# Down product of a float32 decoder trunk: two more pairs multiplied with seven products, four pairs with their lows made by an adding DMA

## The reference, cut to what matters

```python
def swiglu(h, w_gate, w_up, w_down):
    return (jax.nn.silu(h @ w_gate) * (h @ w_up)) @ w_down
# per layer i:
x = x + mixed                       # attention part
h = rmsnorm(x, ffn_norm[i])
x = x + swiglu(h, ffn_w_gate[i], ffn_w_up[i], ffn_w_down[i])
```

## Time and profile before

| what | value |
|---|---|
| median of 3 runs | 2079.42 us (2079.38 to 2079.92) |
| the profiled execution, its own time | 2080.89 us |
| its span | 2079.1 us |
| PE, DVE, ACT, POOL busy, share of the span | 100%, 85%, 70%, 5% |
| granted TensorE clock | 1.0 in the whole span |
| down product of layer 0 | 781.1 to 1012.3 us |
| down product of layer 1 | 1844.4 to 2075.3 us |

### The profile page before, as it was taken

One profiled execution on the slowest core, in us unless ns is written; L12 is line 12 of the kernel. 1 busy time (PEld: TensorE's weight loads), 2 busy tenths in 40 slices (PEclk: granted clock), 3 DMA queues, 4 the chain that ended last, 5 costly groups with the idle time before them and its releaser, 6 DMA issues.

```text
span 2079.1 us, 28758 instructions
## 1 busy us (share of the span) xinstructions
PE 2073.4 (100%) x9652; PEld 1712.0 (82%) x9652; DVE 1764.8 (85%) x2367; ACT 1462.7 (70%) x1993; POOL 99.9 (5%) x79
## 2 busy tenths in 40 slices
PE   9999999999999999999999999999999999999999
PEld 8888888888888888888888888888888888888887
DVE  5775658899999999999767677777999999999998
ACT  6677647677887777766657676666787788777665
POOL 1111000000000000000010101000000000000000
PEclk9999999999999999999999999999999999999999
DMA  8686547787888786665667777676788788876654
GB/s 286 214 229 190 172 164 219 218 260 238 236 254 253 232 237 216 209 207 182 213 217 222 244 211 246 223 226 222 230 240 258 233 240 245 251 223 212 207 184 157
DMA packets 340217, 463.68 MB, mean 223 GB/s; under 512 B 134576, under 2 KB 137360, under 8 KB 340112
## 3 DMA queue, kind: packets, MB, share of 16 engines
q1 hardware_dynamic: 333936, 441.31, 66.5%
q0 software_dynamic: 6080, 20.99, 6.2%
q10 hardware_dynamic: 96, 0.03, 0.0%
HBM read 408.27 MB, written 2.10 MB: 197 GB/s over the span
## 4 chain that ended last, share of the span: by engine, by line
PE 98%; ACT 1%; DMA 1%; DVE 0%; issue 0%; ACTq 0%; POOLq 0%
PE acc L2079 16%; PE work L2079 16%; PE work L2081 16%; PE work L2080 16%; PE acc L2081 16%; PE acc L2080 16%; PE work L2260 1%; PE work L2298 1%; DMA low_b<-raw 1%; PE work L2210 0%; PE work L2271 0%; ACT w_hi L1347 0%; PE work L2305 0%; PE acc L2068 0%; DVE w_lo L1649 0%; PE work L2274 0%
## 5 line engine op out<-in xcount | busy, mean ns | idle before, releaser
L1649 DVE TENSOR_TENSOR w_lo<-raw,w_hi 128x1024 fp32r<-128x1024 f32 x716 | 807.0, 1142 | 84.0 <-ACT w_hi L1347 78.2
L1347 ACT ACTIVATE w_hi<-raw 128x1024 fp32r<-128x1024 f32 x716 | 691.8, 990 | 224.2 <-PE work L2081 132.7
L2079 PE MATMUL work<-w_hi,xT_hi 128*128 128x512 f32 x1194 | 464.9, 389 | 0.0
L2081 PE MATMUL work<-w_hi,xT_lo 128*128 128x512 f32 x1194 | 464.6, 389 | 0.0
L2080 PE MATMUL work<-w_lo,xT_hi 128*128 128x512 f32 x1194 | 464.5, 389 | 0.0
L1347 ACT ACTIVATE w_hi<-sums 128x1024 fp32r<-128x1024 f32 x210 | 220.6, 1059 | 189.5 <-PE work L2081 123.4
L2079 PE MATMUL acc<-w_hi,xT_hi 128*128 128x512 f32 (+1 forms) x905 | 352.4, 389 | 0.5 <-DVE w_lo L1649 0.5
L2081 PE MATMUL acc<-w_hi,xT_lo 128*128 128x512 f32 (+1 forms) x905 | 349.0, 386 | 0.0
L2080 PE MATMUL acc<-w_lo,xT_hi 128*128 128x512 f32 (+1 forms) x905 | 349.0, 386 | 0.0
L1649 DVE TENSOR_TENSOR w_lo<-sums,w_hi 128x1024 fp32r<-128x1024 f32 x210 | 252.9, 1220 | 33.1 <-ACT w_hi L1347 32.5
L2079 PEld LDWEIGHTS work<-w_hi,xT_hi 128*128 128x128 f32 x1194 | 224.1, 188 | 47.0 <-DVE w_lo L1649 0.4
(11 more groups left out here) (209 smaller groups left out, 2438.9 us busy)
## 6 DMA issues: line engine op xcount, KB each, us to landing
raw<-in_ffn_w_down_dram SPq DMA_DIRECT2D x176, 512.0 KB, 4.7
raw<-in_ffn_w_gate_dram SPq DMA_DIRECT2D x160, 512.0 KB, 4.3
raw<-in_ffn_w_up_dram SPq DMA_DIRECT2D x160, 512.0 KB, 5.2
raw<-in_odd_w_in_dram SPq DMA_DIRECT2D x48, 1024.0 KB, 5.6
raw<-in_even_w_in_dram SPq DMA_DIRECT2D x32, 1024.0 KB, 5.9
raw<-in_even_w_out_dram SPq DMA_DIRECT2D x16, 1024.0 KB, 5.0
raw<-in_odd_w_out_dram SPq DMA_DIRECT2D x16, 1024.0 KB, 7.3
low_a<-raw POOLq DMA_DIRECT2D x20, 512.0 KB, 5.8
```

What stands on the lines that cost most here:

```text
L1347: act.activation(w_hi[:, s, 0:out], src, ACT.Copy).then_inc(hi_ready, 1)
L1649: dve.tensor_tensor(w_lo[:, s, 0:out], src, w_hi[:, s, 0:out].bitcast(F32), ALU.subtract).then_inc(lo_ready, 1)
L2079: pe.matmul(out_ps, x_hi, wh, start=start, stop=False)
L2081: return pe.matmul(out_ps, x_lo, wh, start=False, stop=stop)
```

## The change

`DOWN_SEVENS` gets one more pair in layer 0's first pass and one more in layer 1's second pass, and several of the others move. A new list `DOWN_ADDED` names four plain pairs (6 and 15 of layer 0's first pass, 5 and 14 of layer 1's second pass) that are done with `added_half`. Their highs and lows lie in the lower halves of `xT_hi` and `xT_lo`. The ring's splits no longer run at a fixed distance: `high` and `low` map each half to the split that is due there, and halves of added pairs take none. All three tables of due times are new (left out below but for their first lines).

```diff
-PARTS = {"seven": ("two", "one", "sums_a", "sums_b"), "eight": ("pair", "pair"), "last": ("first", "second")}
+PARTS = {"seven": ("two", "one", "sums_a", "sums_b"), "eight": ("pair", "pair"), "added": ("pair", "pair"), "last": ("first", "second")}
...
-DOWN_SEVENS = (((5, 8, 11, 14, 16, 18, 21), (9, 11, 13, 15, 18)), ((5, 8, 11, 14, 16, 18, 21), (5, 8, 11, 13, 15, 18)))
+DOWN_SEVENS = (((5, 8, 10, 12, 14, 17, 19, 21), (9, 11, 13, 15, 18)), ((5, 8, 11, 14, 16, 18, 21), (4, 7, 9, 11, 13,
+               16, 18)))
+DOWN_ADDED = (((6, 15), ()), ((), (5, 14)))
...
+NEGATE_DOWN = ((-8, 0), (-6, 1), (-5, 2), (-4, 3))
...
+        down_hi = xT_hi[:, 0:8, :].rearrange("p (t a) s -> p t (a s)", t=2)
+        down_lo = [xT_lo[:, 4 * i:4 * i + 4, :].rearrange("p a s -> p (a s)") for i in range(2)]
...
+                at_once = [starts[p][q] + i for p in range(2) for q, of in enumerate(DOWN[layer][p]) if of == "added" for i in range(2)]
+                length = starts[1][-1] + len(PARTS["last"])
+                ring = [at for at in range(length) if at not in at_once]
+                kinds = [kind for pairs in DOWN[layer] for of in pairs if of != "added" for kind in PARTS[of]]
+                turns = [at - SPLIT for at in range(SPLIT)] + ring
+                high = {turns[i] + 1: kind for i, kind in enumerate(kinds + AHEAD * ["plain"])}
+                low = {at + 1: kind for at, kind in high.items()}
+
                 def jobs(h, base, raw):
 
 
+                    for p in range(2):
+                        for q in DOWN_ADDED[layer][p]:
+                            for at, step in NEGATE_DOWN:
+                                if starts[p][q] + at == h:
+                                    k = DOWN_PAIRS * p + q
+                                    negate(k, step, raw + 2 * k - n.raw.c, True)
+                                    if step == 3:
+                                        e.passed()
...
                 for i, (q, of, cols) in enumerate(rest):
-                    pair_chunk(layer, q, cols, of, sum(r for r, _ in before[-RAW:]) - 2, (w_down, w_down))
-                    before.append((len(PARTS[of]), False))
+                    added = sum(by_dma for _, by_dma in before[1 - RAW:]) if before[-RAW][1] else None
+                    pair_chunk(layer, q, cols, of, sum(r for r, _ in before[-RAW:]) - 2, (w_down, w_down), added=added, by_dma=of == "added")
+                    before.append((0 if of == "added" else len(PARTS[of]), of == "added"))
...
-                pool.dma_start(added_lo[i][:, :].bitcast(F32), raw[:, (FIRST_SLOT + k) % RAW, i * HALF:(i + 1) * HALF],
+                pool.dma_start((down_lo if down else added_lo)[i][:, :].bitcast(F32), raw[:, (FIRST_SLOT + k) % RAW, i * HALF:(i + 1) * HALF],
                                accum_op=ALU.add).then_inc(low_added[i], 16)
...
-                    act.activation(added_lo[i][:, :], src, ACT.Copy, scale=-1.0).then_inc(negated, 1)
+                    act.activation((down_lo if down else added_lo)[i][:, :], src, ACT.Copy, scale=-1.0).then_inc(negated, 1)
                 else:
-                    act.activation(added_hi[:, i, :], src, ACT.Copy).then_inc(rounded, 1)
+                    act.activation((down_hi if down else added_hi)[:, i, :], src, ACT.Copy).then_inc(rounded, 1)
...
-            def added_half(i, kt, start, held):
+            def added_half(i, kt, start, held, staged, begins):
...
                 pe.wait_ge(low_added[i], n.lows.value(1, unit=16))
+                if staged is None:
+                    x_hi, x_lo, his, los = xT_hi[:, kt, :], xT_lo[:, kt, :], added_hi, added_lo
+                else:
+                    x_hi, x_lo, his, los = stage_hi[:, 2 * staged + kt, :], stage_lo[:, 2 * staged + kt, :], down_hi, down_lo
+                    if begins:
+                        pe.wait_ge(slo_ready, n.taken.value(1))
```

More of the change, by code:

```diff
@@ L293, in decoder_kernel @@
     HALVES = (4 + 8 * 8 + 2 * 4 * 8 + 3 * CG * 8 + 2 * (2 * 8 + (FB - 1) * len(RING))
-              + sum(len(PARTS[of]) for passes in DOWN for half in passes for of in half))
+              + sum(len(PARTS[of]) for passes in DOWN for half in passes for of in half if of != "added"))
     assert DOWN_PAIRS == FK // 2 and all(passes[0][-1] == "seven" for passes in DOWN) and FB % 2
@@ L738, in make_sums, with negate @@
                         n.sums.c += 1
-                def negate(k, step, more):
-                    e.negate(k, step, more)
+                def negate(k, step, more, down=False):
+                    e.negate(k, step, more, down)
                     if step < 2:
@@ L851, in jobs @@
                             if sum_at[u][step] == h:
-                                before = starts[units[u - 1][0]][units[u - 1][1]] + len(PARTS["seven"]) if u else 0
-                                make_sums(step, h + AHEAD - before, raw + 2 * (DOWN_PAIRS * p + q) - n.raw.c)
+                                before = ring.index(starts[units[u - 1][0]][units[u - 1][1]]) + len(PARTS["seven"]) if u else 0
+                                make_sums(step, sum(at <= h for at in low) - before, raw + 2 * (DOWN_PAIRS * p + q) - n.raw.c)
                         if form_at[u][3] == h:
@@ L876, in down @@
                                 e.direct_out(1, 0)
-                            ahead = dict(hi=kinds[h + AHEAD], lo=kinds[h + AHEAD - 1], staged=n.taken.c % STAGED, begins=i == 0)
+                            ahead = dict(hi=high.get(starts[p][0] + h), lo=low.get(starts[p][0] + h), staged=n.taken.c % STAGED, begins=i == 0)
                             if what == "seven":
@@ L883, in down @@
                                 half(kt=i, start=(q, i) == (0, 0), held=(q, i) == (0, 0),
-                                     direct_stop=p == 0 and (q, i) == (DOWN_PAIRS - 2, 1), **ahead)
+                                     direct_stop=p == 0 and (q, i) == (DOWN_PAIRS - 2, 1),
+                                     by_dma=i if what == "added" else None, **ahead)
                             if closes and i in (1, 2):
@@ L929, in feed_forward @@
                 joint(range(FIRST_SPOT, len(SPOTS)), staged_first, more=False)
[L930 to L931 removed]
+                base, raw = n.half.c, (n.raw.c - 4) // (2 * RAW) * (2 * RAW) + 4
                 down(0, first_pass, base, raw)
                 down(1, second_pass, base, raw)
+                n.ups_ahead = False
                 if layer == 1:
@@ L1313, in nat_words, with negate @@
                 last.then_inc(n_split, 1)
-            def negate(k, i, more):
+            def negate(k, i, more, down):
                 if i >= 2:
@@ L1578, in direct_out, with negate @@
                     act.activation(hid[:, 1, :], work[3][:, :], ACT.Copy).then_inc(direct_free, 1)
-            def negate(k, step, more):
+            def negate(k, step, more, down):
                 n, i = e.n, (0, 1, 1, 0)[step]
@@ L2132, in added_half @@
                         rows = slice(m * P, (m + 1) * P)
-                        last = three(work[2 - 2 * w + m], xT_hi[:, kt, rows], xT_lo[:, kt, rows], wh, wl, start, False)
+                        last = three(work[2 - 2 * w + m], x_hi[:, rows], x_lo[:, rows], wh, wl, start, False)
                 last.then_inc(half_used, 1)
@@ L2177, in half @@
                 if by_dma is not None:
-                    return added_half(by_dma, kt, start, held)
+                    return added_half(by_dma, kt, start, held, staged, begins)
                 s = n.ring.slot(SPLIT)
```

18 lines of the change are left out of this document (7 added, 11 removed), and 25 rows, old and new, of tables (FORM_AT, STAGE_AT, SUM_AT).

## The result

The changed kernel takes **2082.97 us** (median; most runs 2081.65 to 2084.69). The kernel before, run beside it, takes 2079.81 us (2079.38 to 2080.81). The ratio is 1.0015, with a 95% interval from 1.0009 to 1.0021: 3.2 us slower, and 1 lies outside the interval, so the change did cost time. The prediction had said 2078.6 us, 0.9 us faster, with 2080.7 us as its upper end. The time is outside that range. It is still within the 0.2% for which 94% was given.

What follows compares the result with a forecast made beforehand. PE, busy throughout, was taken as the bound. Terms of -1.36 (matmuls), +0.4 (layer 0's dense stretch), 0 (layer 1's) and +0.1 us (lows) sum to -0.86, from 2079.42 to 2078.6 us; range 2077.6 to 2080.7.

Steps and rivals of the forecast that it cites:

- The matmuls: Both down products: two more seven-product pairs, 27 for 25, make six matmuls fewer on PE, -1.36 us.
- the old wait: PE's wait for a split behind pair 5 of layer 1's second pass, some 0.25 us; expected to be gone.
- Layer 1's dense stretch: Layer 1's second pass, seven-product pairs 7, 9, 11, 13: taken as 0 us, bounds -0.25 and +1.1.
- DVE beside POOL's issues: DVE isn't held while POOL issues the eight added DMAs: price 0, other bound eight times 0.85 us.
- So four lows cost +0.1 us: PE's waits for the lows of the four added pairs, both layers: +0.1 us, bounds 0 and 2.0.
- ACT's lag, the copy and POOL's issue (0.85 us) leave some 10 to 11 us: Time left of 12.9 us for an added pair's low to land, against landings of 6.4 to 10.6 us.
- No transpose lies beside the four new pairs: Down products: the transpose beside the worst earlier wait for a low has no counterpart at the added pairs.
- lows landing in 6 to 9 us: Sign that the prediction is right, for the lows of the added pairs in the down products.
- Nothing is late: Said of SP's loads behind added pairs; also a rival: no new wait, old wait gone, 2077.8 us, 20%.
- the dense stretch of layer 0, +0.4 us: First pass, seven-product pairs 8, 10, 12, 14: DVE falls back, PE waits 0.4 us, bounds 0 and 1.8.
- The lows are late: Rival: the lows of each of four added pairs come 0.5 us late, 2080.5 us, 9%.
- The added pair empties the ring: Rival: DVE enters dense stretches behind layer 0's pair 6 and layer 1's pair 5 without lead; 2086.3 us, 5%.

Runs made afterwards that it cites:

- e3: The changed kernel with the last merge of the hidden states on ACT moved from pair 12 to pair 16, in both layers: 2083.19 us.
- e6: The changed kernel with ACT's two low copies for layer 0's pair 15 issued 9 and 8 halves ahead, not 8 and 6: 2082.11 us.
- e10: e9 with the later merge of e3, the earlier copies of e6 and pair 17's sums due at 39, 40, 40: 2081.52 us.
- e9: The changed kernel with five due times of DVE in layer 0's first pass moved: 2083.51 us.
- e11: e10 with DVE's weight sums in layer 0's first pass on only 32 of 512 columns, the rest left out: 2079.36 us.
- e4: The changed kernel with layer 0's pairs 6 and 15 plain again, its eight seven-product pairs kept: 2082.19 us.
- e5: The changed kernel with layer 0's old seven-product pairs and tables (two sums earlier), pairs 6 and 15 still added by DMA: 2079.17 us.
- e7: The changed kernel with layer 0's pair 15 plain again, pair 6 still added: 2081.54 us.
- e2: Layer 0's down product as in the changed kernel, layer 1's as before: 2083.50 us, 3.48 more than the kernel before.
- f2: A label that the text given doesn't define; no change or time is given under it.

## Why the prediction was wrong, step by step

**Right.** The matmuls: 9646, and layer 1 alone gives the 0.68 us and the old wait of 0.25 us. Layer 1's dense stretch costs nothing, as taken. DVE beside POOL's issues is not held: in layer 0's first pass, with four of them, none of its splits of 1024 columns lasts over 1.226 us. DVE's average is near what was worked out, 217.1 and 220.1 us. ACT is 3.4 and 7.2 us busier than in the earlier trace rows, against 6.4; in layer 0 the same window now holds less of the work.

**The step that failed most: "So four lows cost +0.1 us".** They cost 1.8 us at pair 15 alone, near the bound of 2.0 that was given for all four. Three of its parts were wrong:
- "ACT's lag, the copy and POOL's issue (0.85 us) leave some 10 to 11 us" allows ACT a lag of at most 1 us. It was 3.5 us at the first copy, and though PE itself lost some 0.5 us on the way, the low had only 8.0 us left: issued at 852.52, wanted at 860.56. This is the part that failed. ACT's queue ahead of the copies was never written out ("one copy more delays them by 1.04 us" was the whole account): it had a wait for DVE's sums and the last merge of the hidden states in it. e3, e6 and e10 show that either move removes the wait.
- "No transpose lies beside the four new pairs" was taken to speak for early landings, and "lows landing in 6 to 9 us" for the sign of being right. There was none, and pair 15's lows landed in 9.3 and 10.4 us. That is inside the 6.4 to 10.6 us of the earlier trace rows, which the sum had allowed for, so by itself it would have been just in time. From 845 to 862 us the loads' queue takes 49.2% of the time of the core's 16 DMA engines and POOL's queue 22.2%, so both are at work on them. The lows of layer 1 and of pair 6 landed in time in after.
- "Nothing is late" was said of SP with landings of 4.7 us from a stretch without adding DMAs. Beside them loads took up to 11.5 us. In after PE doesn't pay for this, since it is late anyway; in e3, e6 and e9 it does, 1.0 to 2.7 us at pair 16. So the two are stacked: who removes only the first sees little of it.

The 1.3 us of the earlier trace rows, from which the bound of 0.5 us a pair comes, were also read wrongly: 0.9 of them are idle time of the weight load, in two waits. PE's own starts in that trace are late at one added pair, by 0.6 us, and the second trace of before has no such wait.

**Mis-sized: the dense stretch of layer 0, +0.4 us.** The mechanism was right, the engine was right, and the place was right; it measured 1.6 us, within the bound of 1.8. The value went by the spare 0.7 us at one split of the old stretch, and the new one didn't have it: PE already waits 0.2 us at pair 5, ahead of it, and 0.4 us at pair 9, behind its first seven-product pair. e11 shows that DVE's work in the stretch decides it. Why the spare time is gone is only argued. That pair 6 frees no ring slot is little of it: in e4, with pair 6 plain, PE waits 1.1 us from pair 9 to 13 in place of 1.4, and 1.25 us at pair 6 itself.

**The common fault: the terms were added as if they were independent.** DVE is late in the dense stretch, so ACT waits for the sums, so the copies are late, so the lows are late, and so the loads behind them. e5 (lows, no dense stretch: no wait for them) and e7 (dense stretch, no lows at 15: 1.6 us of the loss gone) are the two halves of this. The range had the same fault: its upper end took the lows at their bound and DVE at its middle value, and both came near their bounds. With 1.8 and 1.6 us in its place, the sum gives +2.0 us, and +1.8 with the old wait gone; the rest of the measured 3.2 is the open part above. The forecast also counted from a median of three runs, 2079.42 us, which lies 0.4 us under that of the 22. That the time still fell within 0.2% is no merit of the mechanism: all the terms are small against 4.2 us.

**The rivals.** "The lows are late" (9%, 2080.5 us) is the nearest, but with one pair late by 1.8 us in place of four by 0.5. "The added pair empties the ring" (5%) priced at 8.3 us what is 1.6 in all, and by e4 the ring's part in that is small. "Nothing is late" holds for layer 1 alone. ACT standing at a load was looked for in layer 1 and came in layer 0.

**The bytes of a low.** The prediction weighed the Trainium skill, DMA: Bandwidth & Descriptors, section "Anatomy of one DMA — SWDGE (gpsimd) path", by which it estimated that 512 KB land in 3.2 us, and went by the trace. The runs bear this out: over all kernels the shortest landing among the lows of the down products was 4.8 us (e6, e11), the longest 10.7 (e2, f2).

## What to carry to other kernels

Where two edits load the same chain of engines, price them together: write out the queue of each engine from the late one to the DMA's issue, and use for a landing the worst case with everything that will then be in flight. A layer that runs without a wait shows little about the spare time of its twin, and a move that frees one layer can cost in the other, as the late merge did (0.8 us): count the waits of every stage that the edit reaches. Of a change with two halves keep the half that pays: here layer 1's gives 1.0 to 1.3 us, and layer 0's takes 3.5 to 4.5.

## What the runs showed of the hardware

- **Adding DMAs slow the loads beside them.** With two of 512 KB in flight, plain loads that take 3.9 to 4.9 us in e7 took 5.4 to 10.2 us in after and up to 11.5 in e9. Issued 3.3 us earlier (e10), the lows took 5.2 and 6.7 us and the loads 5.7 to 7.8. Why these differ so much isn't settled.
- **A gap of 2.9 us between starts was followed by a lower clock.** In `e3_late_merge`, windows before and behind the gap (columns as above, granted clock third from the end):

```profile
860.00:865.00 5.00, 5.00 (x24) 4.14 (x23) 1.55 (x2) 1.32 (x3) 0.00 (x0) 1.00 0.86 289
868.90:873.10 4.20, 4.20 (x12) 3.34 (x13) 4.04 (x9) 1.10 (x2) 0.00 (x0) 0.61 0.94 296
```

  Some eight matmuls start 0.43 us apart in place of 0.227, the rate of 1.2 in place of 2.4 GHz, which cost 1.6 us on top of the wait. The gaps of up to 1.8 us in the down products of the other kernels weren't followed by this.
- **A DVE instruction on 8 columns still took 0.16 us**, against 0.286 on 128.
